# Values of the second attention computed token by token, with the order of several waits and the masks changed

## The reference

```python
hn = rms_norm(x, norm_g)
proj = hn @ w_in                      # q, k, v, f_logit, g_fox
q = rms_norm(q, q_gain); k = rms_norm(k, k_gain)      # per head of 64
o_moba = moba_attention(q[:, :4], k[:, :4], v[:, :4], slopes[N_DIL:])
o_fox = forgetting_attention(q[:, 4:10], k[:, 4:10], v[:, 4:10], f_logit)
o_dil = dilated_attention(q[:, 10:], k[:, 10:], v[:, 10:], slopes[:N_DIL])
y_moba = rms_norm(to_bsd(o_moba), ...)
y_fox = rms_norm(to_bsd(o_fox), ...) * sigmoid(g_fox)
y_dil = rms_norm(to_bsd(o_dil), ...)
x = x + concat(y_moba, y_fox, y_dil) @ w_out
```

## Time and profile before

| what | value |
|---|---|
| median of 3 runs | 1466.76 us |
| lowest, highest of them | 1466.6, 1767.67 us |
| the profiled execution | 1466.56 us |
| its span | 1464.7 us |
| TensorE busy | 1435.7 us (98%) |
| VectorE, ScalarE, GpSimd busy | 849.8, 604.8, 304.3 us |
| moved from and to memory | 128.33 MB, 88 GB/s in the mean |

### The profile page before, as it was taken

How to read it: one execution, slowest core, us unless ns; L and a number is a source line. 1 busy time by engine, 2 the same in 40 slices (tenths; PEclk the granted TensorE clock), 3 DMA queues, 4 the chain that set the end, 5 groups by cost and what they waited for, 6 DMA issues and landing times.

```text
span 1464.7 us, 23335 instructions
## 1 busy us (share of the span) xinstructions
PE 1435.7 (98%) x9213; PEld 1237.3 (84%) x9213; DVE 849.8 (58%) x1276; ACT 604.8 (41%) x911; POOL 304.3 (21%) x287
## 2 busy tenths in 40 slices
PE   8999999999999999999999999999999999999999
PEld 8999999999998978988987777777677888888887
DVE  6888644457465543553454647897877534344355
ACT  6552677643343221232224345666645313233230
POOL 2660343300115612650453000002103000000000
PEclk9999999999999999999999999999999999999999
DMA  5212111124312332223234132101133322323231
GB/s 204 76 57 88 59 59 58 59 87 146 102 58 87 101 100 87 94 93 101 86 101 136 38 102 72 58 30 58 44 115 103 109 91 98 105 86 100 93 96 70
DMA packets 35849, 128.33 MB, mean 88 GB/s; under 512 B 4085, under 2 KB 4469, under 8 KB 35633
## 3 DMA queue, kind: packets, MB, share of 16 engines
q1 hardware_dynamic: 34608, 122.18, 25.2%
q10 hardware_dynamic: 864, 4.33, 0.8%
q0 software_dynamic: 288, 0.57, 0.1%
HBM read 124.92 MB, written 2.10 MB: 87 GB/s over the span
## 4 chain that ended last, share of the span: by engine, by line
PE 69%; DVE 12%; ACT 8%; POOL 7%; issue 3%; DMA 0%; DVEq 0%; ACTq 0%; SPq 0%; POOLq 0%
PE ps L1918 60%; DVE w_lo L946 2%; POOL gate_conv L1736 2%; POOL conv_tmp L1839 2%; ACT w_hi L392 2%; DVE rot L950 2%; PE ps L1977 1%; POOL phase_tmp L1736 1%; PE ps L2414 1%; PE ps L2389 1%; PE ps L2353 1%; ACT conv_tap L516 1%; DVE rot L1202 1%; POOL gate_conv L1836 1%; PE ps L1983 1%
## 5 line engine op out<-in xcount | busy, mean ns | idle before, releaser
L946 DVE TENSOR_TENSOR w_lo<-w_raw,w_hi 128x1024 fp32r<-128x1024 f32 (+2 forms) x225 | 293.6, 1306 | 181.0 <-ACT w_hi L392 180.2
L1918 PE MATMUL ps<-h_hi,w_hi 128*128 128x512 f32 (+3 forms) x1208 | 347.5, 335 | 5.5 <-DVE qk L950 1.8
L1918 PE MATMUL ps<-h_hi,w_lo 128*128 128x512 f32 (+3 forms) x1208 | 336.8, 326 | 0.0
L1918 PE MATMUL ps<-h_lo,w_hi 128*128 128x512 f32 (+3 forms) x1208 | 336.4, 326 | 0.0
L392 ACT ACTIVATE w_hi<-w_raw 128x1024 fp32r<-128x1024 f32 (+2 forms) x226 | 231.3, 1032 | 175.4 <-PE ps L1918 164.7
L1918 PEld LDWEIGHTS ps<-h_hi,w_hi 128*128 128x128 f32 x1208 | 203.6, 188 | 37.7 <-issue 12.2
L1918 PEld LDWEIGHTS ps<-h_lo,w_hi 128*128 128x128 f32 x1208 | 203.3, 188 | 20.9 <-issue 2.6
L1918 PEld LDWEIGHTS ps<-h_hi,w_lo 128*128 128x128 f32 x1208 | 203.3, 188 | 19.5
L1918 PE MATMUL ps<-f_hi,w_hi 128*128 128x256 f32 (+1 forms) x488 | 129.5, 319 | 0.0
L1918 PE MATMUL ps<-f_hi,w_lo 128*128 128x256 f32 (+1 forms) x488 | 129.5, 319 | 0.0
L1918 PE MATMUL ps<-f_lo,w_hi 128*128 128x256 f32 (+1 forms) x488 | 129.4, 319 | 0.0
(11 more groups left out here) (371 smaller groups left out, 2179.6 us busy)
## 6 DMA issues: line engine op xcount, KB each, us to landing
w_raw<-w_units SPq DMA_DIRECT2D x227, 512.0 KB, 3.3
x<-x_t ACTq DMA_DIRECT2D x1, 2112.0 KB, 8.2
out<-out_tile SPq DMA_DIRECT2D x7, 256.0 KB, 2.0
x<-x_t ACTq DMA_DIRECT2D x3, 528.0 KB, 9.1
x<-x_t ACTq DMA_DIRECT2D x2, 264.0 KB, 4.6
consts<-consts SPq DMA_DIRECT2D x1, 320.0 KB, 6.8
b_step<-ssm_b SPq DMA_DIRECT2D x1, 256.0 KB, 10.4
c_step<-ssm_c SPq DMA_DIRECT2D x1, 256.0 KB, 11.2
```

The source lines that it names most:

```text
L946: Dv.do(v.tensor_tensor(wlo[:, s % RING, 0:w], raw[:, s % RING, 0:w], f32(whi[:, s % RING, 0:w]), ALU.subtract), lo_ready)
L1918: ins = mm(o, wt[:, s % RING, w], xt[:, kx, c0:c0 + n], start=(b == 0 and a == 0), stop=(b == len(blocks) - 1 and a == 2))
```

## The change

1. **Values token-major.** The eight value units are repacked: unit j of a half holds, for two of the eight k tiles, 512 value columns each. TensorE takes a 128x128 block of h (tile k, 128 tokens) as the stationary operand and 512 columns of weights as the moving one, for four token tiles in four banks. The first half runs over four units at once as the tiles of h come; then the gate unit G0, then the forget unit, then the second half. There is no `v2T`, no transpose of values; the row scale is transposed (four of 4x128) and copied to `rcol`, and ScalarE evacuates each bank with it as a scale per partition. `parts_sum` stands behind the first block of G0.
2. **Low part of the fourth unit** within `residual` at tile 6.
3. **Gated output:** the first two sigmoids wait for the first unit only.
4. **Last chunk's down units:** the first two are done without their last tile, then the last tile of each.
5. **Masks, heads 0 to 9:** the masks of token tiles 0 and 2, in one bank, are one matmul with 256 columns.
6. **Masks, dilated heads:** the logarithms are in units of `LOG_UNIT = ln 2 / 665`, so that ln 2 and ln 3 become 665 and 1054, which need no low part; half the mask matmuls go. The query norm and the bias are scaled to the same unit, and the exponential has `scale=LOG_UNIT`. Its bias must be scaled: a small ScalarE copy `nms` of two maxima, twice per head, with a fence.
7. **Output projection:** `split_hi` comes first in the loop.

The diff, cut to its core:

```diff
-            act.wait_ge(unit_done, U_MERGE)
             for m in range(CT):
                 s = (U_GLU + m // 2) % 2
+                if m % 2 == 0:
+                    act.wait_ge(unit_done, U_GLU + m // 2 + 1)
...
-            split_hi(U_V2 + 4)
+            def v2_evac(half):
+
+                for b, bank in enumerate(VB_BANK if half else VA_BANK):
+                    c = slice(half * SEQ, half * SEQ + SEQ)
+                    ins = dn.activation(V[:, b, c], PS[:, bank, :], ACT.Identity, scale=rcol[:, 4 * b:4 * b + 1])
...
+            split_hi(U_G0)
             rsqrt(4, SEQ)
...
+            split_hi(U_F2)
+            split_hi(vb_unit(0))
+            act.wait_ge(sem("rc_mm"), 1)
+            A.do(dn.activation(rcol, PS[:, 3, 0:16], ACT.Copy), sem("rc_ready"))
+            A.fence()
+            act.wait_ge(unit_done, U_V2 + 4)
+            v2_evac(0)
+            split_hi(vb_unit(1))
+            split_hi(vb_unit(2))
+            split_hi(vb_unit(3))
...
+            split_hi(U_QK2 + 1)
+            act.wait_ge(unit_done, U_QK2)
+            v2_evac(1)
...
+                    if h >= N_MOBA + N_FOX:
+                        if t in (T_ORDER[0], T_ORDER[2]):
+                            act.wait_ge(sem("max_ready"), 4 * h + (2 if t == T_ORDER[0] else 4))
+                            two_of = slice(4 * hh + t % 2, 4 * hh + 4, 2)
+                            A.do(dn.activation(nms[:, two_of], nm[:, two_of], ACT.Copy, scale=LOG_UNIT))
+                            A.fence()
...
             for j in range(KT // 2):
+                split_hi(U_OB + j + LOOK)
                 act.wait_ge(sem("x3_even"), j + 1)
...
-                split_hi(U_OB + j + LOOK)
...
+                    if m == 6 and unit is not None:
+                        split_lo(unit)
...
-            for j in range(KT - 1):
-                down(s0 + j, 0, fahi, falo, PS[:, 2 * ((s0 + j) % 2), :], sem("fa_lo") if j == 0 else None, f0, tiles)
+            for first in (True, False):
+                for j in range(2):
+                    s, o = s0 + j, PS[:, 2 * ((s0 + j) % 2), :]
+                    if first:
+                        begin(s)
+                    for k in range(tiles - 1) if first else (tiles - 1,):
...
-            def v2_transposes(j):
...
+            def v2_block(s, b, k, banks, xt, wts, last=False, free=None):
+
+                for t in range(4):
+                    if free is not None and t == 2:
+                        pe.wait_ge(*free)
+                    for wt in wts:
+                        ins = mm(PS[:, banks[t], :], xt[:, k, P * t:P * t + P], wt[:, s % RING, b * SEQ:b * SEQ + SEQ],
+                                 start=(k == 0 and xt is h2hi and wt is whi), stop=(k == KT - 1 and xt is h2lo))
...
+            for k in range(KT):
+                s = U_V2 + k // 2
...
+                pe.wait_ge(sem("h3_hi"), k + 1)
+                v2_block(s, k % 2, k, VA_BANK, h2hi, (whi, wlo))
+                if k % 4 == 3:
+                    four_sums(4, SEQ, k, sqp)
+                pe.wait_ge(sem("h3_lo"), k + 1)
+                v2_block(s, k % 2, k, VA_BANK, h2lo, (whi,), k % 2 == 1)
...
+            def row_columns(b):
+                if b == 0:
+                    parts_sum(4, SEQ)
+                if b == 5:
+                    pe.wait_ge(sem("rs_ready"), 5)
+                    for t in range(4):
+                        ins = nc.tensor.transpose(PS[:, 3, 4 * t:4 * t + 4], rs[0:4, P * t:P * t + P], ident[0:4, 0:4])
+                    ins.then_inc(sem("rc_mm"), 1)
...
-                            for k in range(2):
-                                mm(PS[:, 2 + 3 * hh + bank, c:c + w], identr[:, :], dilr[:, k, P * (3 - t):SEQ],
-                                   start=(t != 2 and k == 0), stop=True, skip_group_check=True)
+                            mm(PS[:, 2 + 3 * hh + bank, c:c + w], identr[:, :], dilr[:, P * (3 - t):SEQ], start=(t != 2), stop=True,
+                               skip_group_check=True)
```

More of the change, by code:

```diff
@@ L44 @@
 NEG = -1e30
+LOG2 = 665
+LOG3 = 1054
+LOG_UNIT = math.log(2.0) / LOG2
 LOOK = 2
@@ L261, in build @@
     Pb = [at(f"probs{j}", [3, SEQ], R + 43008 + 6144 * j) for j in range(2)]
-    vT2 = [at(f"v2T{j}", [SEQ], R + 43008 + 2048 * j) for j in range(2)]
     qtmp = at("qk_tmp", [SEQ], R + 55296)
@@ L308, in build @@
     esel = small[:, 300:300 + KT]
-    nm, rsum, rinv = (small[:, 32 + 8 * j:40 + 8 * j] for j in range(3))
+    rcol = small[:, 100:116]
+    nm, rsum, rinv, nms = (small[:, 32 + 8 * j:40 + 8 * j] for j in range(4))
     def sum_weight(norm):
@@ L964, in rstd @@
                 sums = PS[:, 4:6, 0:n // 2] if n != SEQ else PS[:, 4, :]
[L965 removed]
+                u = {2: U_FFN}.get(norm)
                 if norm < 5:
@@ L1358, in _, with residual @@
             half_rstd(1, TW, 1)
-            def residual(gain, n, c0, ready, hi, lo, pre, thi, tlo):
+            def residual(gain, n, c0, ready, hi, lo, pre, thi, tlo, unit=None):
                 def low(m):
@@ L2291, in _ @@
                 s0 += KT
-            for j in range(KT - 1):
-                down(s0 + j, 0, fahi, falo, PS[:, 2 * ((s0 + j) % 2), :], sem("fa_lo") if j == 0 else None, f0, tiles)
+            for first in (True, False):
[4 more added lines that the diff above has]
+                    for k in range(tiles - 1) if first else (tiles - 1,):
+                        if j == 0:
+                            pe.wait_ge(sem("fa_lo"), f0 + k + 1)
+                        w = slice(k * P, k * P + P)
+                        mm(o, whi[:, s % RING, w], fahi[:, k, :], start=(k == 0), stop=False)
+                        mm(o, whi[:, s % RING, w], falo[:, k, :], start=False, stop=False)
+                        ins = mm(o, wlo[:, s % RING, w], fahi[:, k, :], start=False, stop=not first)
+                    if not first:
+                        ins.then_inc(unit_done, 1)
+            for j in range(2, KT - 1):
+                down(s0 + j, 0, fahi, falo, PS[:, 2 * ((s0 + j) % 2), :], None, f0, tiles)
             last = 2 * ((U_V2 - 1) % 2)
@@ L2427, in out_part @@
                      [(k, k) for k in range(KA)])
-            wide(qk_unit(0, 0))
-            wide(qk_unit(0, 1))
+            for w in range(2):
+                pe.wait_ge(lo_ready, qk_unit(0, w) + 1)
+                unit(qk_unit(0, w), 0, h2hi, h2lo, [(PS[:, qk_unit(0, w) % 2, :], 0, SEQ)])
+            pe.wait_ge(evacuated, U_QK2 + 1)
             pe.wait_ge(lo_ready, gate_unit(1) + 1)
@@ L2614 @@
     count = (d >= 0) * ((d <= 128) * 1 + ((d % 4 == 0) & (d <= 512)) + ((d % 16 == 0) & (d <= 2048)))
-    dil = np.where(count > 0, np.log(np.maximum(count, 1)), NEG).astype(np.float32)
+    dil = np.choose(count, (NEG, 0.0, LOG2, LOG3)).astype(np.float32)
     def diagonal(re, im):
```

165 lines of the change are left out of this document (75 added, 90 removed).

## The result

The changed kernel takes 1450.49 us (median of four runs, 1450.19 to 1451.67), the kernel before 1466.78 beside it. The ratio estimated from the runs of both is 0.9894, with a 95% interval of 0.9882 to 0.9907 (the two medians alone give 0.9889): faster, and clear of the noise, but by less than 2%. The forecast was 1451.0, and "within 2%" was the case that got 0.96. The profiled execution took 1451.67, with a span of 1449.9, so 14.8 less span than before.

What follows compares the result with a forecast made beforehand. TensorE was taken as the bound, busy 1435.7 of 1464.7 us. Savings 2.4 + 2.9 + 5.5 + 4.9 - 2.2 + 2.1 = 15.6 took 1466.56 to 1451.0 us, range 1446 to 1458.

Steps and rivals of the forecast that it cites:

- within 2%: Whole kernel: the changed time differs from the kernel before by no more than 2%; chance 0.96.
- Gated output, 2.4: State-space branch: TensorE's waits for a sigmoid, 1.27, and for low parts, 0.84, both go; 2.4 us saved.
- Last chunk, 2.9: Last feed-forward chunk: reordered down units fill the wait and the half-speed stretch goes, new wait 0.7; 2.9 us saved.
- Values, 5.5: Values: transposes 3.6, two waits 1.7 and partial-sums wait 0.4 go, four small transposes cost 0.25; 5.5 us saved.
- Masks, 4.9: Attention heads: joined masks save 1.0, dropped low halves of dilated masks 3.9, all on TensorE; 4.9 us saved.
- the second rival: Attention: VectorE and ScalarE set the pace, so neither mask saving passes, 1458.5, or half binds, 1454.8; chance 0.15.
- Scaled maxima, -2.2: Dilated heads: scaled copies and a later first exponential delay probabilities by 1.6; 1.6 and 0.6 pass in two pairs, 2.2 lost.
- Output projection, 2.1: Output projection: TensorE's waits for low weights, 0.65 and 1.12, go with the high part moved first; 2.1 us saved.
- the first rival: TensorE: a half-speed stretch stays or comes anew; one costs 1.6, two 3.2, giving 1452.6 to 1454.2; chance 0.18.
- The table loads: Dilated heads, a rival: ScalarE loads tables around the small copies, 24 loads of 1.28, giving 1482; chance 0.02.
- slower by over 2%: Whole kernel: the change makes it more than 2% slower, said to need the table loads; chance 0.02.

Runs made afterwards that it cites:

- the experiment: Changed kernel each time: under gated output, old sigmoid wait back, 1453.65 us; under output projection, `split_hi` in its old place, 1452.64; for transposes, 32 put back, 1453.93.
- the identity: Changed kernel with the logarithm unit in the mask matmul's stationary identity and no scaled maxima: 1448.62 us, ratio 0.9885.

## Why the prediction was right, step by step

**Gated output, 2.4.** Right in mechanism and nearly in size: 2.65 between the profiles, 2.6 by the experiment. Both waits hung on the one semaphore. The 0.15 added per bracket for the restart was a little small.

**Last chunk, 2.9.** The profiles agree (2.8) and so does the new wait, 0.71. But the step mis-sized what a run gains. 1.6 of the 2.9 was the half-speed stretch, and I took it for something that every execution has. The runs show 1.0 to 1.1 in executions without one, from both sides. The forecast named 1.3 "if the stretch comes all the same"; what is true is that it came in some executions before, and comes in far fewer with the new order (4 of 43 against 19 of 41). By these counts, an estimate, the order is worth 1.0 and about a third of a stretch in the mean of many executions.

**Values, 5.5.** Right: 5.45 in the profiles, 5.5 alone. Transposes 3.6 (measured 3.7), and the swap of the operands costs nothing per matmul. The transposed row scale costs 0.66 - 0.23 = 0.43 from 834.39 to 835.05, where I took 0.25, near the upper bound. The wait for it did not come, and the order of four units per block covers the other waits.

**Masks, 4.9.** The dilated part, 3.9, measured 4.1. The joined masks were put at 1.0, "nearer to the upper end": their own rows give 0.8, and only 0.4 to 0.7 reaches the end. The step that failed is that all of it passes: a part of what TensorE saves in these pairs it then spends on waiting for VectorE's chain (in two of the five pairs, 0.16 each). That the second rival, attention paced by VectorE and ScalarE, goes no further is shown by the dilated masks, whose saving passes whole.

**Scaled maxima, -2.2.** Measured -1.6 to -1.7. The delay of the exponentials was 1.33, not 1.6: the three copies between the exponentials cost 0.17 each and not 0.25. The first exponential is 0.83 later, close to the 0.6 for the second maximum and the 0.25 for its own copy that were forecast. I said that the delay passes in the second dilated pair; it did (1.3). In the first I put 0.6 and it was 0.2. The place of the wait was wrong: I expected 1.21 to grow to nearly 3 at ScalarE's copy of the probabilities. It stayed 1.21, and the wait stands 6.3 us earlier, 0.80 at the query square (L2403), which ScalarE makes behind the same exponentials; another 0.3 goes in the transposes before it, whose row is 2.62 long in after and 2.34 with the identity. TensorE then comes to the copy as much delayed as ScalarE does, so that bracket stays as it was.

**Output projection, 2.1.** 2.45 between the profiles and 2.4 by the experiment: mechanism right, the restarts again dearer than 0.15 each, some 0.3.

**The rivals.** A half-speed stretch came anew in the profiled execution of after, and not in the median: 1451.67 against 1450.49. It stands behind a wait that both kernels have, not behind the one at the end of the dilated heads that the first rival named and that did not grow. The second rival holds for two of the five joined masks and for no more. The table loads did not come: L797 and L874 have eight and seven loads in after as their lines had before, and the small copies of the earlier trace rows's kind take 0.20. The price of that rival was wrong in one place: its 1482 is 1.1% above the kernel before, so it was no case of "slower by over 2%", as the prediction has it.

Put together by the lower groups: 5.5 + 1.1 + 2.6 + 2.4 + 4.1 + 0.6 - 1.7 = 14.6, of 14.65 measured. Within what these sets can tell the parts add up, so none leans on another. The forecast's 15.6 has 1.8 too much for the last chunk and 0.4 too much for the joined masks, against 0.5 too much taken off for the maxima, 0.5 too little for the restarts at two places and 0.2 too little for the dilated masks. These errors partly cancel. The rest, 1.0, is hidden by luck: the runs of before in this comparison all lay in the upper group and three of the four of after in the lower one, 1466.78 - 1450.49 = 16.3. Between lower groups the forecast of 15.6 stands against 14.65.

## What to carry to other kernels

Take a wait away by giving the engine that waits the work that stands behind it, and cost the new order by the next wait that it creates: here the new wait came out within 0.1 us of the forecast at the chunk, and at the values none came. Before a gain is credited to a clock that rises, look at the list of run times; where they lie in groups as far apart as the stretch is dear, the stretch belongs to the execution, and the groups have to be compared one by one, and their shares of the executions beside them. When a factor has to go in somewhere, put it in a constant operand of an engine's product, not in dependent small copies on the path: these cost 1.6 here, with the later maximum that the first of them waits for, and the scaled identity at most 0.15.

## What the runs showed of the hardware that was not expected

**A wait brings a half-speed stretch in some executions and not in others.** In the thirteen profiles of this case, a stretch of half speed (the granted clock is 0.50 in the mean from 772 to 774 in the kernel before) in the middle of the span was seen behind the 1.79 wait at 770 (before; and the old order put back, at 767) and behind the 1.79 wait at 115 (after; and with the old sigmoids), and in the nine others nowhere, although both waits stand in the kernel with the values alone. By the groups each costs 1.4 to 1.9. It was seen behind waits of 1.8 only; behind those of 1.64 to 1.72 near 525, in twelve of the profiles, and behind those at the start of the kernel (2.19 in after, up to 2.38 in others), the clock stayed at 1.00. The wait at 770 brought it far oftener than the one at 115, as the shares of the executions show. What decides within an execution is open: no run here tells it.

The Trainium skill (TensorE: Matmul & The Clock Gate, Part 1) has half speed as the resting state of the array that activity releases. By that rule I had thought the stretch tied to the wait; the trace agrees that it comes only behind one, and the pair of windows 0.53 and 1.00 behind equal waits shows that the wait alone does not settle it.

**Here the role of the operands does not matter.** 0.23 from start to start for 128x128 stationary and 512 moving columns, whether the weights are stationary or the activations (858.89 to 859.12).

**Four small transposes cost as much as four full ones.** Four transposes of 4x128 lengthen the stream by 0.43, four full ones of 128x128 by 0.46 (a set in the experiment), so their size sets little of the price. That it is the price of leaving the stream of large matmuls is a guess; no run tested it.
